# A two-layer decoder trunk on one Trainium2 core: where the first FFN's loop builds the S5 matrices

## The chip, the cores and the metric

The kernel runs on one core of one Trainium2 chip. The metric is the device time of one execution in microseconds. A core has five engines that run their own instruction streams and meet only at semaphores: TensorE (PE, with its weight loads as PEld), VectorE (DVE), ScalarE (ACT), GpSimd (POOL) and SyncE (SP).

## The reference, cut to what matters

Sixteen meta tokens are put ahead of 1024 tokens of width 1024, so T = 1040. Two layers follow, each with a mixer and a SwiGLU FFN, both between RMS norms. Layer 0 mixes with four gated-DeltaNet heads and four stick-breaking heads, layer 1 with a diagonal complex state-space model (S5) and a GLU.

```python
def swiglu_ffn(x, w_gate, w_up, w_down):
    return (jax.nn.silu(x @ w_gate) * (x @ w_up)) @ w_down

for i in range(DEPTH):
    hn = rms_norm(h, norm_mix_pre[i])
    m = deltanet_stickbreak_mixer(hn, ...) if i % 2 == 0 else s5_mixer(hn, ...)
    h = h + rms_norm(m, norm_mix_post[i])
    hn = rms_norm(h, norm_ffn_pre[i])
    h = h + rms_norm(swiglu_ffn(hn, ...), norm_ffn_post[i])
```

The FFN width is 2816. The S5 mixer has 64 groups of 16 channels, each driving 64 complex states. Its matrices (input and output matrices, phases, and the products of the two for each lag inside a chunk of 8 steps) depend on parameters alone, not on the tokens, so they can be built at any time before the mixer of layer 1.

## The kernel before, in words

Everything is written by engine: one function body each for SyncE, GpSimd, TensorE, ScalarE and VectorE, with the semaphores written out by hand. What an engine does, it does in the order of its body.

Activations lie feature-major, 128 features by T tokens, and the tokens are cut into three cuts of 352, 344 and 344 (CUTS). Each weight is streamed from HBM in slabs of 128 x 1024 (SyncE, L521) and split by GpSimd into a high and a low fp32r part (L554, L558); each product is three matmuls, high by high, high by low, low by high (L582 to L584).

The FFN goes over the 2816 hidden features in 11 turns (PAIRS) of two blocks of 128. A turn has six steps: step st works on cut st // 2 and block st % 2. On TensorE a step is `hidden(i, c, f)` with c = st // 2 and f = st % 2: the gate and up products of that block and cut, 48 matmuls into two of banks 0 to 3. ScalarE then takes silu of the gate (L1475), VectorE multiplies it by the up product (L2068), ScalarE copies that into act_hi (L1479), and VectorE makes act_lo of the rest (L2071). Behind the six steps TensorE makes the down products, `down(i, c)` for each cut, eight groups of six matmuls into three banks in turn (4, 5, 6); VectorE adds each group to acc (L2081) and so frees its bank.

The FFN of layer 0 (called with layer 0) carries the building of the S5 matrices. It has one channel tile (m = i - 1) in each of the turns i = 1 to 8 of its loop; the FFN of layer 1 has the same loop without it. Per turn:

- VectorE: behind step 0 `build_in` (the input matrices zb["m"], two parts), behind step 1 `build_out` (waits until the set of the turn before is stored), behind step 2 `build_phases`, behind step 5 `build_k`: it waits for the lag products in bank 7 and adds a diagonal term (L2198). The additions of the down products stand behind that.
- TensorE: `build_turn(m, 0)` transposes the first part into bank 7 (four transposes, L647), `build_turn(m, 1)` the second, `build_k` makes the lag products (eight matmuls of 32 columns, L655 and L656), all in bank 7. Each of the latter two waits for `s5["win"]`, that is, until ScalarE has evicted what bank 7 holds.
- ScalarE: `build_win(m, 0)` and `build_win(m, 1)` evict the transposed parts from bank 7 (L1493); the first also waits for the store of the set of the turn before. At the end of the turn `store_build` starts the DMA of the set (L1499) and eight DMAs of the lag products (L1501), and `load_tab` the next tables (L1486).

On TensorE the order of a turn is: groups 0, 1, 2, first transposes, group 3, second transposes, group 4, lag products, group 5, down products. On ScalarE the first eviction stands behind step 3, the second behind step 4.

Of the kernel before, what the change touches and what calls it, by code (L numbers as in the profile page):

```python
# [282 lines left out]
def trunk(nc, xT, wstream, small_in, const_in, s5_in, outT):  # L283
    with ExitStack() as ctx:
# [149 lines left out]
        def split_value(name, i, j):  # L434

            return first_slab(name) + i * len(slots_of(name)[1]) + j + 3
# [138 lines left out]
        def _(pe):  # L575
            mm = pe.matmul

            def gemm(out, slot, k, xk, cut, first, last, hi=x_hi, lo=x_lo):

                a, n = cut  # L580
                wk = slice(k * P, k * P + P)
                mm(out[:, 0:n], w_hi[:, slot, wk], hi[:, xk, a:a + n], start=first, stop=False)  # L582
                mm(out[:, 0:n], w_hi[:, slot, wk], lo[:, xk, a:a + n], start=False, stop=False)  # L583
                return mm(out[:, 0:n], w_lo[:, slot, wk], hi[:, xk, a:a + n], start=False, stop=last)  # L584
# [40 lines left out]
            def norm_sum(r, c, m):  # L625


                n = CUTS[c][1]
                e = norm_event(r, c, m)
                if e:  # L630
                    pe.wait_ge(nm_log, e)
                for k in range(KT):
                    if k % 4 == 0:

                        pe.wait_ge(nm_square, 2 * e + k // 4 + 1)
                    last = mm(norm_sums[:, 0:n], ones, nv["sq"][:, k, 0:n], start=(k == 0), stop=(k == KT - 1))  # L636
                last.then_inc(nm_sum, 1)
# [3 lines left out]
            def build_turn(m, part):  # L641

                if part == 0:
                    pe.wait_ge(s5["m"], m + 1)
                pe.wait_ge(s5["win"], 2 * m + part + 1)
                for q in range(QP):
                    last = pe.transpose(bank[7][:, q * P:q * P + P], zb["m"][part][:, q, :], ident)  # L647
                last.then_inc(s5["win_t"], 1)

            def build_k(m):  # L650

                pe.wait_ge(s5["win"], 2 * m + 3)
                for q in range(QP):
                    o = bank[7][:, q * 2 * G_CH:(q + 1) * 2 * G_CH]
                    mm(o, zb["m"][0][:, q, :], zb["cc"][0][:, q, :, :], start=True, stop=False)  # L655
                    last = mm(o, zb["m"][1][:, q, :], zb["cc"][1][:, q, :, :], start=False, stop=True)  # L656
                last.then_inc(s5["k"], 1)

            def ffn(layer, r):

                name = f"ffn{layer}"
                base = layer * PAIRS

                def hidden(i, c, f):

                    pe.wait_ge(split_done, split_value(name, i, 2 * f + 1))
                    step = (base + i) * 6 + 2 * c + f

                    pe.wait_ge(act_f32, step + 1)
                    for s in (2 * f, 2 * f + 1):  # L670
                        for k in range(KT):
                            last = gemm(bank[s], s, k, k, CUTS[c], k == 0, k == KT - 1)
                    last.then_inc(gu_done, 1)

                def down(i, c):

                    pe.wait_ge(split_done, split_value(name, i, 5))
                    pe.wait_ge(act_ready, (base + i) * 6 + 2 * c + 2)
                    for m in range(KT):
                        pe.wait_ge(down_free, (base + i) * 24 + c * 8 + m + 1)  # L680
                        b = bank[4 + (8 * c + m) % DOWN_BANKS]
                        slot = 4 + m // 4
                        for kk in range(2):
                            last = gemm(b, slot, kk * 4 + m % 4, kk, CUTS[c], kk == 0, kk == 1, act_hi, act_lo)
                        last.then_inc(down_done, 1)

                def pair(i):
                    for c in range(3):
                        hidden(i, c, 0)
                        hidden(i, c, 1)  # L690

                end = PAIRS - 1
                pe.wait_ge(x_ready, 3 * r + 1)
                hidden(0, 0, 0)
                norm_sum(r, 2, 0)
                hidden(0, 0, 1)
                pe.wait_ge(x_ready, 3 * r + 2)
                hidden(0, 1, 0)
                norm_sum(r, 2, 1)
                hidden(0, 1, 1)  # L700
                pe.wait_ge(x_ready, 3 * r + 3)
                hidden(0, 2, 0)
                hidden(0, 2, 1)
                for c in range(3):
                    down(0, c)
                with pe.Fori(1, end - 1) as i:
                    for c in range(3):
                        hidden(i, c, 0)
                        if layer == 0 and c == 1:
                            build_turn(i - 1, 0)  # L710
                        if layer == 0 and c == 2:
                            build_k(i - 1)
                        hidden(i, c, 1)
                        if layer == 0 and c == 1:
                            build_turn(i - 1, 1)
                    for c in range(3):
                        down(i, c)
                pair(end - 1)
                down(end - 1, 0)
                down(end - 1, 1)  # L720

                hidden(end, 0, 0)
                hidden(end, 0, 1)
                down(end - 1, 2)
                hidden(end, 1, 0)
                down(end, 0)
                hidden(end, 1, 1)
                norm_sum(r + 1, 0, 0)
                hidden(end, 2, 0)
                down(end, 1)  # L730
                if r + 1 < 4:
                    norm_sum(r + 1, 0, 1)
                hidden(end, 2, 1)
                norm_sum(r + 1, 1, 0)
                down(end, 2)
                if r + 1 == 4:
                    norm_sum(4, 2, 0)
# [339 lines left out]
        def _(act):  # L1077
# [7 lines left out]
            def norm_load(r, c):  # L1085

                a, n = CUTS[c]
                if r == 4 and c == 2:
                    act.wait_ge(nm_stored[0], 16 * 7)
                elif c == 2:  # L1090
                    act.wait_ge(x_ready, 3 * r + 1)
                elif r > 0:
                    act.wait_ge(x_ready, 3 * (r - 1) + (3 if c == 0 else 2))
                act.dma_start(nv["h"][c % 2][:, :, 0:n], stream_in[r][:, :, a:a + n]).then_inc(nm_loaded[c % 2], 16)
# [369 lines left out]
            def ffn(layer, r):  # L1464
# [19 lines left out]
                def load_tab(m):  # L1484

                    act.dma_start(zb["tab"], s5_tab[:, m, :]).then_inc(s5["tab_loaded"], 16)  # L1486

                def build_win(m, part):

                    act.wait_ge(s5["win_t"], 2 * m + part + 1)  # L1490
                    if part == 0:
                        act.wait_ge(s5["set_stored"], 16 * m + 16)
                    A(zb["win"][part].rearrange("p q s -> p (q s)"), bank[7], ACT.Copy).then_inc(s5["win"], 1)  # L1493
# [21 lines left out]
                if layer == 0:  # L1515
                    act.sem_inc(s5["win"], 1)
                    act.sem_inc(s5["set_stored"], 16)
                    act.sem_inc(s5["k_stored"], 16 * CH)
                    act.wait_ge(x_ready, 3 * r + 3)
                    load_tab(0)  # L1520
                    with act.Fori(1, end - 1) as i:
                        for st in range(6):
                            step(i, st)
                            if st in (3, 4):
                                build_win(i - 1, st - 3)
                        store_build(i - 1)
                        load_tab(i)
                    for st in range(3):
                        step(end - 1, st)
                    act.wait_ge(s5["set_stored"], 16 * KT + 16)  # L1530
                    act.wait_ge(s5["k_stored"], 16 * CH * (KT + 1))
                    act.wait_ge(s5["tab_loaded"], 16 * KT + 16)
                    norm_load(r + 1, 0)
                    norm_load(r + 1, 1)
                    for st in range(3, 6):
                        step(end - 1, st)
                else:
                    norm_load(r + 1, 0)
                    norm_load(r + 1, 1)
                    with act.Fori(1, end) as i:  # L1540
                        for st in range(6):
                            step(i, st)
# [28 lines left out]

            act.sem_inc(down_done, 1)
            ffn(0, 1)


# [806 lines left out]
```

## Time and profile before

| | us |
|---|---|
| median of 3 runs | 3452.55 |
| lowest and highest run | 3443.03, 3460.74 |
| span of the profiled execution | 3441.6 |
| TensorE busy | 2945.9 (86%) |
| VectorE busy | 1343.9 (39%) |
| GpSimd busy | 944.0 (27%) |
| ScalarE busy | 746.9 (22%) |

The profile records one execution; its span runs from the first to the last instruction. The granted TensorE clock is given as a share of full speed. The loop of the first FFN lies at about 1260 to 1895 us of the span, that of the second at about 2738 to 3290.

### The profile page before, as it was taken

How to read it: one execution, taken by the hardware profiler on the slowest of the kernel's cores; microseconds unless marked ns; L12 is line 12 of the kernel's file. 1: busy time of each engine (PE TensorE's matmuls, PEld its weight loads, DVE VectorE, ACT ScalarE, POOL GpSimd, SP SyncE). 2: the span in 40 equal slices, each digit the busy share in tenths (PEclk: the TensorE clock that was granted, in tenths of full speed). 3: DMA queues.
4: the chain of work that ended last, by engine and by line, in shares of the span. 5: the costliest groups of instructions: out<-in, count | busy, mean ns of one | idle time of the engine just before them, and what ended most of it. 6: DMA issues, size and time to landing. Idle time of an engine off the chain costs nothing.

```text
span 3441.6 us, 45325 instructions
## 1 busy us (share of the span) xinstructions
PE 2945.9 (86%) x17797; PEld 2782.7 (81%) x17797; DVE 1343.9 (39%) x2281; ACT 746.9 (22%) x1270; POOL 944.0 (27%) x390
## 2 busy tenths in 40 slices
PE   3999978776668899999999987755997999999996
PEld 2999966664448799999999986645996999999995
DVE  2664055544571544443434234063025332233223
ACT  3321133434562320000000033112033000000002
POOL 2344200000003333333434330400531544354430
PEclk8999988987778999999999998877998999999998
DMA  4222510000102211111122213686111211111101
GB/s 154 75 98 92 114 44 25 25 25 19 37 19 70 87 57 63 63 63 63 66 71 85 87 46 75 139 193 158 62 58 58 83 49 49 37 49 49 49 25 66
DMA packets 175482, 236.23 MB, mean 69 GB/s; under 512 B 56480, under 2 KB 140960, under 8 KB 173088
## 3 DMA queue, kind: packets, MB, share of 16 engines
q1 hardware_dynamic: 66064, 133.42, 13.0%
q10 hardware_dynamic: 109328, 101.54, 9.8%
q8 instruction: 65, 1.06, 0.1%
q14 instruction: 25, 0.20, 0.0%
HBM read 172.37 MB, written 62.55 MB: 68 GB/s over the span
## 4 chain that ended last, share of the span: by engine, by line
issue 34%; PE 32%; POOL 11%; DVE 9%; DMA 6%; ACT 5%; ACTq 2%; SPq 1%; POOLq 0%; DVEq 0%
POOL w_hi L554 7%; PE psum L582 7%; PE psum L583 6%; PE psum L584 6%; POOL w_lo L558 3%; DMA stage<-wstream 3%; PE psum L636 3%; DVE area L1701 2%; PE psum L825 2%; PE psum L817 1%; DVE area L2036 1%; PE psum L936 1%; DVE area L1706 1%; DMA area<-xT 1%; PE psum L833 1%
## 5 line engine op out<-in xcount | busy, mean ns | idle before, releaser
L582 PE MATMUL psum<-x_hi,w_hi 128*128 128x344 f32 (+2 forms) x3600 | 1176.8, 327 | 56.9 <-DVE x_lo L1724 34.3
L583 PE MATMUL psum<-x_lo,w_hi 128*128 128x344 f32 (+2 forms) x3600 | 1170.1, 325 | 0.0
L584 PE MATMUL psum<-x_hi,w_lo 128*128 128x344 f32 (+2 forms) x3600 | 1165.3, 324 | 0.0
L554 POOL TENSOR_TENSOR w_hi<-stage,const 128x1024 fp32r<-128x1024 f32 x193 | 471.8, 2445 | 2386.9 <-PE psum L584 2365.6
L582 PEld LDWEIGHTS psum<-x_hi,w_hi 128*128 128x128 f32 x3600 | 690.8, 192 | 62.3 <-DVE x_lo L1724 32.7
L583 PEld LDWEIGHTS psum<-x_lo,w_hi 128*128 128x128 f32 x3600 | 689.8, 192 | 1.9
L584 PEld LDWEIGHTS psum<-x_hi,w_lo 128*128 128x128 f32 x3600 | 690.8, 192 | 0.0
L558 POOL TENSOR_TENSOR w_lo<-stage,w_hi 128x1024 fp32r<-128x1024 f32 x193 | 475.8, 2465 | 15.1
L582 PE MATMUL psum<-act_hi,w_hi 128*128 128x344 f32 (+1 forms) x1056 | 347.8, 329 | 36.9 <-DVE area L2081 29.3
L2068 DVE TENSOR_TENSOR area<-area,psum 128x352 f32<-128x352 f32 (+1 forms) x132 | 68.0, 515 | 723.7 <-ACT area L1475 723.7
L584 PE MATMUL psum<-act_hi,w_lo 128*128 128x344 f32 (+1 forms) x1056 | 342.1, 324 | 0.0
L583 PE MATMUL psum<-act_lo,w_hi 128*128 128x344 f32 (+1 forms) x1056 | 341.3, 323 | 0.0
L1475 ACT ACTIVATE area<-psum 128x352 f32<-128x352 f32 (+1 forms) x132 | 60.7, 460 | 1280.0 <-PE psum L584 1280.0
L2081 DVE TENSOR_TENSOR area<-area,psum 128x344 f32<-128x344 f32 (+1 forms) x480 | 243.1, 515 | 187.2 <-PE psum L584 185.3
L582 PEld LDWEIGHTS psum<-act_hi,w_hi 128*128 128x128 f32 x1056 | 201.3, 191 | 45.4 <-DVE area L2081 36.4
L636 PE MATMUL psum<-area,const 128*128 128x344 f32 (+1 forms) x384 | 127.9, 491 | 89.8 <-ACT area L1111 89.8
L583 PEld LDWEIGHTS psum<-act_lo,w_hi 128*128 128x128 f32 x1056 | 203.4, 193 | 0.1
L584 PEld LDWEIGHTS psum<-act_hi,w_lo 128*128 128x128 f32 x1056 | 201.2, 191 | 0.0
L636 PEld LDWEIGHTS psum<-area,const 128*128 128x128 f32 x384 | 77.8, 207 | 132.0 <-issue 101.8
L1786 DVE TENSOR_TENSOR area<-area 128x512 f32<-128x512 f32 (+6 forms) x298 | 158.7, 587 | 40.6 <-ACT area L1240 32.4
L2071 DVE TENSOR_TENSOR act_lo<-area,act_hi 128x352 fp32r<-128x352 f32 (+1 forms) x132 | 103.4, 783 | 78.2 <-ACT act_hi L1479 78.2
L1701 DVE SCALAR_TENSOR_TENSOR area<-area,small 128x344 f32<-128x344 f32 (+1 forms) x96 | 73.8, 840 | 125.3 <-ACT area L1125 125.3
(214 smaller groups left out, 2571.8 us busy)
## 6 DMA issues: line engine op xcount, KB each, us to landing
stage<-wstream SPq DMA_DIRECT2D x193, 512.0 KB, 3.3
s_set<-area ACTq DMA_DIRECT2D x8, 1860.0 KB, 7.0
proj<-area ACTq DMA_DIRECT2D x28, 520.0 KB, 2.7
area<-proj ACTq DMA_DIRECT2D x40, 256.0 KB, 4.4
resid<-area ACTq DMA_DIRECT2D x6, 1376.0 KB, 6.0
area<-resid ACTq DMA_DIRECT2D x6, 1376.0 KB, 8.3
area<-proj ACTq DMA_DIRECT2D x12, 520.0 KB, 4.6
area<-xT ACTq DMA_DIRECT2D x4, 1376.0 KB, 8.3
```

What stands on the lines that cost most here:

```text
L554: pool.tensor_tensor(per_block(w_hi[:, slot, :]), per_block(stage[:, h, :]), all_ones, ALU.mult).then_inc(high_split, 1)
L558: pool.tensor_tensor(w_lo[:, slot, :], stage[:, h, :], w_hi[:, slot, :].bitcast(F32), ALU.subtract).then_inc(split_done, 1)
L582: mm(out[:, 0:n], w_hi[:, slot, wk], hi[:, xk, a:a + n], start=first, stop=False)
L583: mm(out[:, 0:n], w_hi[:, slot, wk], lo[:, xk, a:a + n], start=False, stop=False)
L584: return mm(out[:, 0:n], w_lo[:, slot, wk], hi[:, xk, a:a + n], start=False, stop=last)
L636: last = mm(norm_sums[:, 0:n], ones, nv["sq"][:, k, 0:n], start=(k == 0), stop=(k == KT - 1))
L825: last = mm(B[1][:, hs], v[s]["u"][:, hs], v[s]["t2"][:, hs], start=True, stop=True)
L1701: last = V.scalar_tensor_tensor(out=acc[:, k, a:a + n], in0=acc[:, k, a:a + n], scalar=small[:, at:at + 1], in1=rr, op0=mul, op1=mul)
L1786: tt = lambda o, a, b, op: ch(V.tensor_tensor(o, a, b, op))
L2068: V.tensor_tensor(f[st % 2][:, 0:n], gate[st % 2][:, 0:n], bank[2 * (st % 2) + 1][:, 0:n], mul).then_inc(act_f32, 1)
L2071: V.tensor_tensor(act_lo[:, st % 2, a:a + n], f[st % 2][:, 0:n], act_hi[:, st % 2, a:a + n].bitcast(F32), sub).then_inc(act_ready, 1)
L2081: last = V.tensor_copy(o, src) if first else V.tensor_tensor(o, o, src, add)
```

## The change

The first eviction on ScalarE moves from behind step 3 to behind step 2, the second from behind step 4 to behind step 3. On TensorE the lag products move from between groups 4 and 5 to behind group 5, ahead of the down products. The transposes stay where they are, and nothing is added or removed. Only the FFN of layer 0 is touched, and of it only the loop of eight turns.

```diff
@@ -708,11 +708,11 @@
                         hidden(i, c, 0)
                         if layer == 0 and c == 1:
                             build_turn(i - 1, 0)
-                        if layer == 0 and c == 2:
-                            build_k(i - 1)
                         hidden(i, c, 1)
                         if layer == 0 and c == 1:
                             build_turn(i - 1, 1)
+                    if layer == 0:
+                        build_k(i - 1)
                     for c in range(3):
                         down(i, c)
@@ -1521,8 +1521,8 @@
                     with act.Fori(1, end - 1) as i:
                         for st in range(6):
                             step(i, st)
-                            if st in (3, 4):
-                                build_win(i - 1, st - 3)
+                            if st in (2, 3):
+                                build_win(i - 1, st - 2)
                         store_build(i - 1)
                         load_tab(i)
```

## Rows read from the trace of the kernel before

**Rows 1.** The page's first row.
```profile
span 3441.6 us, 45325 instructions
```

**Rows 2.** Table by stretch: stretch, length, busy us (instructions) by engine, clock, DMA, GB/s.
```profile
1300.00:1895.00 595.00, 553.06 (x3427) 546.03 (x3426) 249.11 (x469) 51.61 (x108) 221.12 (x92) 0.97 0.20 69
2738.00:3290.00 552.00, 549.35 (x3459) 547.01 (x3459) 159.10 (x288) 45.97 (x97) 232.46 (x97) 1.00 0.14 46
```

**Rows 3.** The same for two turns; then line L1499, its issues: ns, first and last.
```profile
1494.80:1573.40 78.60, 73.36 (x459) 72.48 (x458) 33.47 (x64) 6.69 (x14) 28.90 (x13) 0.98 0.20 69
1573.40:1653.50 80.10, 74.86 (x457) 73.98 (x457) 33.40 (x64) 6.69 (x14) 28.76 (x13) 0.96 0.20 67
...
L1499 ACTq DMA_DIRECT2D s_set<-area x8: 362/362/377, 1335.7 to 1887.3; - x8
```

**Rows 4.** TensorE's waits, 1300 to 1895, then 2738 to 3290: us, times, longest.
```profile
PE psum L655 <- ACT area L1493: 17.4, 8, 2.2
PE psum L647 <- ACT area L1493: 16.8, 8, 2.1
PE psum L582 <- DVE area L2081: 7.7, 8, 1.0
...
PE psum L582 <- DVE area L2081: 2.7, 8, 0.3
```

**Rows 5.** Timeline of TensorE around the second transposes: start, length, idle before it.
```profile
1544.14 0.32 PE L584 MATMUL psum<-x_hi,w_lo 128*128 128x344 f32 x1
1546.56 0.66 PE L647 MATMUL psum<-const,area 128*128 128x128 f32 x4 [2.10 <-ACT area L1493]
1546.97 0.41 PE L582 MATMUL psum<-x_hi,w_hi 128*128 128x344 f32 x1
...
1547.85 0.49 PE L584 MATMUL psum<-x_hi,w_lo 128*128 128x344 f32 x1
...
1551.27 0.32 PE L584 MATMUL psum<-x_hi,w_lo 128*128 128x344 f32 x1
...
1551.90 0.32 PE L582 MATMUL psum<-x_hi,w_hi 128*128 128x344 f32 x1
```

**Rows 6.** Timeline of TensorE around the lag products.
```profile
1556.00 0.32 PE L584 MATMUL psum<-x_hi,w_lo 128*128 128x344 f32 x1
1558.50 0.41 PE L655 MATMUL psum<-area 128*128 128x32 f32 x2 [2.18 <-ACT area L1493]
...
1560.30 0.40 PE L582 MATMUL psum<-x_hi,w_hi 128*128 128x344 f32 x1
```

**Rows 7.** Timeline of TensorE, end of group 5 and the fourth down group.
```profile
1567.79 0.32 PE L584 MATMUL psum<-x_hi,w_lo 128*128 128x344 f32 x1
...
1570.71 0.32 PE L584 MATMUL psum<-act_hi,w_lo 128*128 128x352 f32 x1
...
1571.99 0.43 PE L582 MATMUL psum<-act_hi,w_hi 128*128 128x352 f32 x1 [0.96 <-DVE area L2081]
```

**Rows 8.** Timeline of ScalarE: copy of step 2, first eviction, silu of step 5.
```profile
1537.64 0.49 ACT L1479 ACTIVATE act_hi<-area 128x344 fp32r<-128x344 f32 x1 [0.66 <-DVE area L2068]
...
1545.93 0.58 ACT L1493 ACTIVATE area<-psum 128x512 f32<-128x512 f32 x1
...
1568.15 0.46 ACT L1475 ACTIVATE area<-psum 128x344 f32<-128x344 f32 x1 [9.70 <-PE psum L584]
```

**Rows 9.** Timeline of VectorE: output matrices, act_lo of step 5, first additions to acc.
```profile
1531.03 3.82 DVE L1786 TENSOR_TENSOR area<-area 128x512 f32<-128x512 f32 x6
...
1569.71 1.27 DVE L2071 TENSOR_TENSOR act_lo<-area,act_hi 128x344 fp32r<-128x344 f32 x1 [0.56 <-ACT act_hi L1479]
...
1571.42 1.38 DVE L2081 TENSOR_TENSOR area<-area,psum 128x352 f32<-128x352 f32 x3 [0.23 <-DVE area L2198]
```

**Rows 10.** Table by stretch, columns as in rows 2: short stretches of two turns.
```profile
1548.00:1550.00 2.00, 2.00 (x9) 2.00 (x8) 0.00 (x0) 0.00 (x0) 0.00 (x0) 0.50 0.00 0
...
1640.00:1643.40 3.40, 3.40 (x14) 3.40 (x13) 0.00 (x0) 0.00 (x0) 3.32 (x2) 0.50 0.48 154
```

## The prediction: what the change does to the time

> **What bounds the kernel now.** I read the page first: a span of 3441.6 us [rows 1]. Then the table by stretch for the loops of the two FFNs. They do the same matrix work in every turn, but only the first carries the S5 building. Over seven turns and a half of the first FFN TensorE is busy 553.06 of 595 us, with a clock of 0.97. Over eight turns of the second it is busy 549.35 of 552 us, with a clock of 1.00, so a turn there takes 69.0 us [rows 2]. The s5_set store is issued once a turn of the first FFN; from its first to its last issue (1335.7 to 1887.3) seven turns take 551.6 us, or 78.8 us each [rows 3]. A single turn takes 78.6 us, and one of them 80.1 us with a clock of 0.96 where the others have 0.98 [rows 3]. So TensorE is the bound of both loops, and a turn of the first is 9.8 us longer. The chain of the whole run names TensorE first; the other engines count here only where TensorE stands still for them.
>
> The view of waits says for whom. In the first FFN TensorE has three waits, each eight times: 17.4 us for the eviction at L1493 ahead of the lag products (L655), 16.8 us for the eviction at L1493 ahead of the second transposes (L647), 7.7 us ahead of a down product (L582) for VectorE's L2081. In the second FFN only the last is left, with 2.7 us [rows 4]. No wait for weights is there.
>
> **What the waits cost.** A matmul's end is modelled, so I count from start to start. Ordinary 344-column matmuls follow each other every 0.157 us (1551.27 to 1551.90, four steps [rows 5]).
> Second transposes: the last gate-and-up matmul starts at 1544.14, the first transpose at 1546.56: 2.42 − 0.16 = 2.26 us lost [rows 5].
> Lag products: 1556.00 to 1558.50: 2.50 − 0.16 = 2.34 us [rows 6].
> Fourth down group: 1570.71 to 1571.99: 1.28 − 0.16 = 1.12 us [rows 7].
> Clock: after the first of these gaps the granted clock falls to 0.50, its lower level of 1.2 GHz [rows 10]. From 1547.85 to 1551.27 TensorE starts 12 matmuls in 3.42 us, one per 0.285 us, where 12 at the upper level (2.4 GHz) take 1.88: 1.54 us lost [rows 5]. This happens in each of the eight turns; in the turn of 80.1 us the clock also falls after the lag products [rows 3, 10], and that turn is 1.5 us longer. So nine falls.
>
> **The change, part by part.**
> 1) The eviction of the first turned matrix goes from behind step 3 to behind step 2 on ScalarE. What it needs are the first transposes, which TensorE issues right behind the group of step 2 in both kernels. ScalarE starts step 2's copy at 1537.64, over a microsecond behind that group; the transposes, which hold TensorE for 0.41 us (1546.56 to 1546.97 for the second ones [rows 5]), are over by then. The copy ends at 1538.13, and the eviction takes 0.58 us: done at about 1538.8. TensorE wants it at 1544.3. So the wait of 2.26 us goes with 5.5 us to spare; today the eviction starts at 1545.93, because it stands behind silu, product and copy of step 3, that is, behind a group that TensorE has just finished [rows 5, 8]. The eviction costs ScalarE nothing: it has no other work until step 3's silu, which must wait for a group that ends at 1544.3.
> The eviction also waits for the s5_set store of the turn before, and now meets that wait one step earlier, with silu 3 queued behind it on ScalarE and step 3's product on VectorE behind that. VectorE's output matrices wait for the same store behind step 1, and start at 1531.03 without idling [rows 9]; the store is long done. Cost 0. From below zero nothing is to be had either.
> 2) The second eviction goes from behind step 4 to behind step 3. It needs the second transposes, which now follow step 3's group at once. It is done about 2.4 us behind that group (today: 1546.51, against a group that ended at 1544.30 [rows 5, 8]).
> 3) The lag products go from ahead of the last gate-and-up group to behind it. They find their matrix some 15 us old, so the wait of 2.34 us goes. The eight small matmuls cost the same 1.80 us (1558.50 to 1560.30 [rows 6]) wherever they stand.
> 4) What this does to the down products. Let H be the end of the last gate-and-up group, 1567.95 today (last start 1567.79 plus 0.16 [rows 7]; silu at 1568.15 [rows 8]). VectorE ends step 5 at 1569.71 + 1.27 = 1570.98, H + 3.0, sums the lag products, and adds three down results from 1571.42, H + 3.5 [rows 9]. The first is added at H + 4.0, and the fourth down group, which needs its bank, stands since H + 2.9. After the change TensorE spends H to H + 1.9 on the lag products, so the fourth group comes up at H + 4.8, behind the add at H + 4.0: the wait of 1.12 us goes too. VectorE now waits for fresh lag products: ready at H + 1.9 plus about 0.2 (the distance from H to silu), while VectorE is free for them at H + 3.0. Margin 0.9 us. The bounds of this item are 0 (all gone) and the whole 1.12 kept; I take 0, since the terms above leave 0.8 us.
> 5) DMAs. The store and the eight s5_k stores wait for the lag sum, which is bound by H + 3.0 in both kernels, so these and the table load behind them keep their place against H. No SyncE queue and no GpSimd instruction is moved. GpSimd may refill its first four slabs from steps 4 and 5 on; the two come 1.9 us closer together. It needs at most 20 us for them (29 us of work on six slabs a turn: 232.46 us in eight turns [rows 2]), and they are wanted only behind the down products, 24 groups of 6 matmuls or 23 us later. The second FFN runs this very order at 69.0 us a turn without a wait for weights [rows 2, 4]. Cost 0.
> 6) Clock. With the gaps gone nothing of the kind that precedes the falls is left: the loop of the second FFN, with a small gap of 0.3 us a turn, holds 1.00 throughout [rows 2, 4]. New is a stretch of 1.8 us with only small matmuls. Today the same stretch stands behind a gap of 2.34 us, and even together they brought a fall in one turn of eight. I take all nine falls as gone; the other end is that eight stay, 12.3 us.
> The Trainium skill, "TensorE: Matmul & The Clock Gate", section "Why this matters for your kernels", puts the danger at idle gaps longer than any of the three here. By it the falls would not come from the gaps, and the change would give back only 45.8 us; the trace of this kernel differs, with the clock at 0.50 right behind a gap of 2.26 us in every turn.
>
> **The sum.** Waits: 8 × (2.26 + 2.34 + 1.12) = 45.8 us. Clock: 9 × 1.54 = 13.9 us. Together 59.7 us, or 7.5 us a turn: 78.8 becomes 71.3. A check from the other side: the second FFN's 69.0, less its own 0.3 of waiting, plus 1.9 for the lag products and 2 × 0.45 for the transposes (0.41 from their first start to the next matmul [rows 5]) gives 71.5. The two agree within 0.2 us a turn.
> Against the profiled execution: 3441.6 − 59.7 = 3381.9 us of span. The runs gave 3443.0 to 3460.7, median 3452.6, which is 11.0 above that span. One profile doesn't show what makes the others longer; I suppose the same of the runs afterwards: 3452.6 − 59.7 = 3392.9 us.
>
> **Rivals.**
> A: the clock still falls once a turn, now behind the lag products or the transposes. For it: in one turn it fell behind the lag products, at 1640 [rows 10]. Against it: that was behind a gap that goes. Gain 45.8 + 1.5 = 47.3 us: 3405 us. Chance 0.13. The same page says, under "Part 4: PE-mode transpose", that transposes don't count as busy for the clock in the way other matmuls do; the trace has transposes right ahead of each of the eight falls, but never without the gap in front.
> B: the down wait stays, because VectorE is late with the sum (the lag products are now fresh and the margin is 0.9 us). Gain 59.7 − 9.0 = 50.7 us: 3402 us. Chance 0.05.
> C: the change doesn't do what it says: another semaphore of the same eviction comes last and both gaps merely move. ScalarE has the eviction at 1545.93 right behind its own copy, not behind something foreign, and VectorE's start at 1531.03 clears the store; both speak against it [rows 8, 9]. Time 3452. Chance 0.03.
> D, slower: VectorE now waits for lag products that are issued only behind the last group, and 24 additions to acc stand behind that wait; with three banks, TensorE's down products stop after three groups. The point: the sum may be late by 0.9 + 0.8 us for nothing; to eat the whole gain of 7.5 us a turn it would have to come 9.2 us late, and 11.3 us for a time 0.5% longer (17 us over 8 turns): 3470 us. It would need eight matmuls of 1.8 us to take over 13. Chance 0.02.
> The forecast itself has 0.77.
>
> **Range and chances.** From 3392.9, downward: the median before carries 11 us over the profiled span, and executions without it would give 3382; upward, A and B end at 3402 to 3405, and the spread of a median of a few runs is some 4 us on top. Range 3379 to 3409. Under 0.5%, or 17 us, a measurement of this kernel can't tell a change from none. Faster by more: the forecast, A and B, 0.95. Within: C, 0.03. Slower: D, 0.02.
>
> **What would show it.** The waits of TensorE for L1493 gone from the first FFN (34.2 us before); the wait for L2081 below 1 us in all; the s5_set stores 71.3 us apart; granted clock 1.00 in the loop's stretches; VectorE's L2198 starting about 3.0 us behind the last gate-and-up matmul, with no idle time ahead of it that ends on TensorE. It would be wrong if VectorE idles there for the lag products, if the clock falls behind them, or if ScalarE's silu 3 starts later against its group than 0.2 us.

## The result and the profile after

The changed kernel takes 3390.5 us (median of four runs, 3387.3 to 3392.9) against 3448.5 us for the kernel before on the same chip: 58 us less by the medians, and a ratio of 0.9825 (95% interval 0.9803 to 0.9847), which is 53 to 68 us. The second time it ran, on another occasion, the ratio was 0.985 (0.9828 to 0.9872), or 44 to 59 us. The profiled executions have spans of 3441.6 and 3385.5 us, 56.1 us apart.

The table by stretch of the changed kernel, for a stretch inside the loop of the first FFN and for eight turns of the second (stretch, length, then busy us and instructions of TensorE, its weight loads, VectorE, ScalarE, GpSimd, then the clock, the DMA share and GB/s):

```profile
1310.00:1820.00 510.00, 510.00 (x3274) 509.74 (x3273) 237.48 (x445) 49.25 (x103) 206.64 (x86) 1.00 0.22 74
2682.00:3234.00 552.00, 549.34 (x3459) 547.00 (x3458) 159.03 (x288) 45.96 (x97) 232.51 (x97) 1.00 0.14 46
```

TensorE is busy for all of 510 us, at the full clock, where it was busy 553 of 595 at 0.97 [rows 2]. The second FFN is as it was. The issues of the s5_set store, once a turn (ns; first and last start in us):

```profile
L1499 ACTq DMA_DIRECT2D s_set<-area x8: 362/362/377, 1329.5 to 1827.1; - x8
```

Seven turns take 497.6 us, or 71.1 us each, against 78.8 [rows 3]. So of the 56.1 us between the two spans 54.0 lie between the first and the last of these issues, and 6.2 ahead of the first, where the rest of the first turn is. Behind the last the changed kernel takes 4.1 us more (1558.4 against 1554.3 us). The view of waits of TensorE, 1230 to 1850 us, which holds the whole loop (who waits for whom: us in all, times, the longest):

```profile
PE psum L582 <- DVE x_lo L1724: 5.9, 1, 5.9
PE psum L582 <- DVE area L2081: 0.3, 1, 0.3
```

Both stand ahead of the loop of eight turns, at 1239.6 and 1259.6 us. The three groups of eight waits of [rows 4] are gone. The timeline of TensorE, first around the end of a turn's gate-and-up groups (start and length in us):

```profile
1539.20 0.32 PE L584 MATMUL psum<-x_hi,w_lo 128*128 128x344 f32 x1
1539.36 0.30 PE L655 MATMUL psum<-area 128*128 128x32 f32 x2
...
1541.06 0.41 PE L582 MATMUL psum<-act_hi,w_hi 128*128 128x352 f32 x1
...
1543.89 0.33 PE L584 MATMUL psum<-act_hi,w_lo 128*128 128x352 f32 x1
1544.06 0.33 PE L582 MATMUL psum<-act_hi,w_hi 128*128 128x352 f32 x1
...
1594.73 0.32 PE L584 MATMUL psum<-x_hi,w_lo 128*128 128x344 f32 x1
1594.89 0.60 PE L647 MATMUL psum<-const,area 128*128 128x128 f32 x4
1595.24 0.41 PE L582 MATMUL psum<-x_hi,w_hi 128*128 128x344 f32 x1
```

The lag products start 0.16 us behind the last gate-and-up matmul, take 1.70 us, and the fourth down group starts at 1544.06, 0.17 us behind the third. The second transposes (1594.89) follow group 3 without a gap. VectorE in the same places:

```profile
1541.11 1.15 DVE L2071 TENSOR_TENSOR act_lo<-area,act_hi 128x344 fp32r<-128x344 f32 x1 [0.56 <-ACT act_hi L1479]
1542.18 0.28 DVE L2198 TENSOR_TENSOR area<-psum,area 128x128 f32<-128x128 f32 x1
1542.69 1.11 DVE L2081 TENSOR_TENSOR area<-area,psum 128x352 f32<-128x352 f32 x2 [0.23 <-DVE area L2198]
```

The end of the last group, H, is 1539.20 + 0.16 = 1539.36. The lag sum starts at H + 2.8 right behind act_lo, without idling for TensorE. The first addition ends at about 1543.2, H + 3.9, and the bank it frees is wanted at H + 4.7. ScalarE, the first eviction of a turn and the next silu:

```profile
1588.23 0.49 ACT L1479 ACTIVATE act_hi<-area 128x344 fp32r<-128x344 f32 x1 [0.66 <-DVE area L2068]
1588.63 0.58 ACT L1493 ACTIVATE area<-psum 128x512 f32<-128x512 f32 x1
1595.08 0.46 ACT L1475 ACTIVATE area<-psum 128x344 f32<-128x344 f32 x1 [5.87 <-PE psum L584]
```

The eviction is over at 1589.2; TensorE wants it at 1594.9, and silu 3 starts 0.19 us behind its group (1594.73 + 0.16), so nothing is held up by the evictions.

### The profile page after: what moved, and what is told of

Same layout as the page of the kernel before. It is cut to its first block, busy times and chain, and to the rows that moved or that the text cites. A ratio compares the mean times of both kernels' runs of the same rounds, so it can differ in the third digit from the quotient of the medians.

```text
span 3385.5 us, 45325 instructions
## 1 busy us (share of the span) xinstructions
PE 2931.3 (87%) x17797; PEld 2770.2 (82%) x17797; DVE 1355.0 (40%) x2281; ACT 746.3 (22%) x1270; POOL 951.1 (28%) x390
## 4 chain that ended last, share of the span: by engine, by line
issue 34%; PE 28%; DVE 12%; POOL 11%; ACT 6%; DMA 6%; ACTq 2%; SPq 1%; POOLq 0%; DVEq 0%
POOL w_hi L554 7%; PE psum L582 5%; PE psum L583 5%; PE psum L584 5%; POOL w_lo L558 3%; DMA stage<-wstream 3%; PE psum L636 3%; DVE area L1778 2%; PE psum L825 2%; DVE area L1701 2%; PE psum L817 1%; DVE area L2036 1%; PE psum L936 1%; DVE area L1706 1%; PE psum L833 1%
## 5 line engine op out<-in xcount | busy, mean ns | idle before, releaser
L2081 DVE TENSOR_TENSOR area<-area,psum 128x344 f32<-128x344 f32 (+1 forms) x480 | 244.5, 514 | 191.7 <-PE psum L584 189.3
```

The lines of the kernel that those rows point to most:

```text
L2081: last = V.tensor_copy(o, src) if first else V.tensor_tensor(o, o, src, add)
```

## The experiments

All ratios are to the kernel before. "Turn" is the distance of the s5_set stores, from the first to the last of eight, over seven. "Falls" are stretches at the lower clock level, counted over the eight turns in the table by stretch, one row for each turn. In that table a turn without a fall has a clock of 1.00, one with a fall 0.98 and one with two 0.96; a fall on the boundary of two rows leaves 0.99 in both. Such a row counts the falls of a turn but doesn't tell behind which gap they come; that takes short stretches behind each gap. Line numbers are those of each kernel: an edit above a line shifts it.

For the kernel before, the prediction's rows have such stretches of two turns only, the fourth and the fifth [rows 5, 10]. Here are the first, second and sixth turn, for each the stretch behind the second transposes and then the one behind the lag products (the second line starts during the last lag products):

```profile
1311.00:1320.00 9.00, 7.94 (x52) 7.66 (x50) 0.51 (x1) 0.46 (x1) 0.98 (x1) 1.00 0.01 2
1322.60:1325.90 3.30, 3.30 (x14) 3.30 (x14) 0.00 (x0) 0.00 (x0) 3.30 (x2) 0.50 0.23 50
1390.90:1394.20 3.30, 3.30 (x13) 3.30 (x12) 0.00 (x0) 0.00 (x0) 0.00 (x0) 0.50 0.00 0
1403.00:1411.00 8.00, 8.00 (x53) 8.00 (x53) 0.00 (x0) 0.02 (x1) 5.92 (x3) 1.00 0.28 91
1706.00:1714.00 8.00, 7.48 (x48) 7.19 (x46) 0.00 (x0) 0.46 (x1) 0.44 (x1) 1.00 0.00 0
1718.50:1721.80 3.30, 3.30 (x13) 3.30 (x13) 0.00 (x0) 0.00 (x0) 3.22 (x3) 0.50 0.51 159
```

Read this way, the nine falls are four behind the second transposes (turns 2 to 5) and five behind the lag products (turns 1 and 5 to 8). The prediction had eight and one. Its count is right and its places are not, and the same misreading stands in the expectations of the next runs.

| kernel | turn us | TensorE waits left in the loop | falls | ratio (95%) |
|---|---|---|---|---|
| before | 78.8 | all three | 9 | 1 |
| changed | 71.1 | none | 0 | 0.9825 (0.9803 to 0.9847) |
| evictions only | 72.7 | L2081 | 0 | 0.9856 (0.982 to 0.9893) |
| lag products only | 74.7 | second transposes | 6 | 0.9927 (0.9898 to 0.9957) |
| first eviction only | 77.4 | lag products, L2081 | 13 | 0.9962 (0.9939 to 0.9985) |
| before, one gap filled | 78.8 | lag products, L2081 | 8 | 0.9999 (0.9977 to 1.0022) |
| before, both gaps filled | 77.1 | L2081 | 0 | 0.9969 (0.9955 to 0.9984) |
| changed, lag products twice | 73.7 | none | 4 | 0.9892 (0.9869 to 0.9915) |
| changed, one copy | 72.9 | L2081 | 0 | 0.9873 (0.9854 to 0.9892) |
| changed, four copies | 82.3 | L2081 | clock 0.94 | 1.0065 (1.0039 to 1.0091) |
| changed, sum three times | 71.1 | none | 0 | 0.9816 (0.9791 to 0.984) |
| changed, sum seven times | 72.3 | L2081 | 0 | 0.9854 (0.9831 to 0.9877) |
| changed, copies behind step 3 | 71.1 | none | 0 | 0.9833 (0.9811 to 0.9854) |

**The changed kernel again**, as the neighbour of the copies and the doubled lag products.

> The changed kernel itself, beside the next three on the same chip, as their reference: 3390 us, a gain of 56 to 60 us.

0.985 (0.9828 to 0.9872), or 52 us at 3452.0 us: a little less than the 56 to 60 expected. Its turn is 71.1 us again.

**The two halves of the change.** Evictions alone:

```diff
-                            if st in (3, 4):
-                                build_win(i - 1, st - 3)
+                            if st in (2, 3):
+                                build_win(i - 1, st - 2)
```

> Only ScalarE's part of the change: both evictions one step earlier, the lag products stay ahead of the last gate-and-up group. Theory (three waits and the clock falls behind them add up): TensorE's two waits for L1493 go, 8 x (2.26 + 2.34) = 36.8 us, the nine falls of the clock go with them, 13.9 us, the wait for L2081 stays (7.7 us in the view of waits). Gain 50.7 us against the kernel before, about 3398 us. Rival (the down wait has to do with the late evictions, not with the place of the lag products): it goes here too and the whole 59.7 us is gained. Rival (the clock falls come from the small matmuls, not from the gaps): gain 37 to 38 us, eight falls stay.

The lag products alone:

```diff
-                        if layer == 0 and c == 2:
-                            build_k(i - 1)
                         hidden(i, c, 1)
                         if layer == 0 and c == 1:
                             build_turn(i - 1, 1)
+                    if layer == 0:
+                        build_k(i - 1)
```

> Only TensorE's part of the change: the lag products behind the last gate-and-up group, the evictions where they were. Theory: the wait ahead of the lag products goes (8 x 2.34) and the wait for L2081 (8 x 1.12), the wait ahead of the second transposes stays (16.8 us) and with it one fall of the clock a turn. Gain 27.7 + 1.5 = 29.2 us, about 3419 us. Rival (the sum on VectorE is late for fresh lag products): L2081's wait stays, gain 20 us.

The waits of TensorE (evictions only; 1300 to 1840 us) and the stores:

```profile
PE psum L582 <- DVE area L2081: 9.7, 7, 1.4
...
L1499 ACTq DMA_DIRECT2D s_set<-area x8: 362/362/382, 1337.8 to 1847.0; - x8
```

The same of the kernel with the lag products moved only:

```profile
PE psum L647 <- ACT area L1493: 14.7, 7, 2.1
...
L1499 ACTq DMA_DIRECT2D s_set<-area x8: 362/362/382, 1342.8 to 1865.8; - x8
```

Each half removes the waits that the theory gives it and no other. The evictions alone end both waits for L1493 but leave the one for L2081; the lag products alone end that one and their own. The evictions bring 6.1 us a turn (8 × 6.1 = 49 us, expected 50.7; 50 us by the ratio), the lag products 4.1 (33 us, expected 29.2; 25 us by the ratio, with an interval of 15 to 35). In the first the down wait has even grown, to 1.4 us where it was 0.96: VectorE's act_lo of step 5 takes 1.69 us there, against 1.27 [rows 9]. The rival in which the down wait hung on the late evictions is out, and so is a late lag sum. In the second six turns of eight still have a fall, all behind the second transposes: three falls fewer than before, where the theory had one fewer. That is most of the 4 us above the expectation.

**The first eviction alone**, where only the wait ahead of the second transposes goes:

```diff
-                            if st in (3, 4):
-                                build_win(i - 1, st - 3)
+                            if st in (2, 4):
+                                build_win(i - 1, st // 2 - 1)
```

> Only the first eviction one step earlier; the second stays behind step 4 and the lag products ahead of the last group. Theory: the wait ahead of the second transposes goes, 8 x 2.26 = 18.1 us, and the eight falls behind it, 12.3 us; the gap of 2.34 us ahead of the lag products and L2081's wait stay. If that gap brings a fall of its own no more often than before (one turn in eight), the gain is 30 us, about 3418 us; if it brings one in each turn, 18 to 20 us. The granted clock by turn tells which.

The gain is 13 us, not 18 to 32, and by the turn 8 × 1.4 = 11. Two of its turns in the table by stretch (the clock is the third number from the end):

```profile
1336.10:1413.50 77.40, 74.68 (x456) 74.18 (x456) 33.13 (x63) 6.70 (x14) 28.25 (x13) 0.96 0.21 70
1490.90:1568.30 77.40, 73.68 (x460) 72.78 (x458) 34.31 (x66) 6.70 (x14) 29.87 (x14) 0.98 0.21 70
```

Five turns have 0.96 and three 0.98: thirteen falls where the kernel before has nine. All thirteen come behind the gap ahead of the lag products, at least one in each turn. Neither expected outcome came: with the first gap gone, the second brings one or two falls in a row. It all adds up nevertheless: 78.8 less the gap of 2.26, with 13 falls instead of 9 over eight turns (+0.5 × 1.54 = 0.8), is 77.3, and 77.4 was measured.

**One gap filled, then both.** This keeps every microsecond of waiting but gives TensorE something to do in it:

```diff
                         hidden(i, c, 1)
                         if layer == 0 and c == 1:
+                            pe.wait_ge(down_free, i * 24 + DOWN_BANKS)
+                            for _n in range(14):
+                                mm(bank[4][:, 0:344], w_hi[:, 0, 0:P], x_hi[:, 0, 352:696], start=True, stop=True)
                             build_turn(i - 1, 1)
```

> The kernel before, with 14 matmuls of 344 columns into an idle bank put on TensorE between group 3 and the second transposes; their results are used by nothing. They take 14 x 0.157 = 2.2 us, the length of the gap. So the gap is filled with work and not a microsecond of waiting is saved. Theory (the gap makes the clock fall): the eight falls behind the second transposes go and nothing else, gain 12.3 us, about 3436 us. Rival (the transposes or the turn's rhythm make it fall, not the gap): no fall goes, no gain.

The ratio is 0.9999: no gain. Timeline of TensorE with the gap filled, and two short stretches of the same turn behind it:

```profile
1552.26 2.36 PE L717 MATMUL psum<-x_hi,w_hi 128*128 128x344 f32 x14
1554.52 0.65 PE L647 MATMUL psum<-const,area 128*128 128x128 f32 x4
1564.91 0.41 PE L655 MATMUL psum<-area 128*128 128x32 f32 x2 [2.18 <-ACT area L1496]
```

```profile
1564.30:1567.70 3.40, 2.79 (x22) 2.79 (x23) 1.12 (x1) 0.56 (x2) 3.32 (x2) 1.00 0.00 0
1567.80:1571.20 3.40, 3.40 (x14) 3.40 (x14) 0.00 (x0) 0.00 (x0) 3.32 (x2) 0.51 0.49 154
```

The fall behind the second transposes is gone as the theory said, but all eight falls now come behind the lag products, where the kernel before has five. They are not one a turn: the first turn has none, the second has two in a row (6.8 us at 0.50), the other six one each. So four falls went and three came. I changed the theory: either gap by itself brings a fall a turn, and the clock comes back only when both go. The second filler stands ahead of the lag products, in addition to the first:

```diff
                         if layer == 0 and c == 2:
+                            for _n in range(15):
+                                mm(bank[4][:, 0:344], w_hi[:, 2, 0:P], x_hi[:, 0, 352:696], start=True, stop=True)
                             build_k(i - 1)
```

> The kernel before with both gaps filled: 14 matmuls of 344 columns ahead of the second transposes, as with one gap filled, and 15 more (2.35 us) ahead of the lag products; their results are used by nothing. No waiting is saved, TensorE only works through it. Theory, as it stands after the run with one gap filled (either gap by itself brings one fall of the clock a turn; the falls go only when both are gone): all falls of the loop go, gain 9 x 1.54 = 13.9 us, about 3438 us, with a turn of 77.0 us. Rival (the small matmuls bring the falls, whatever stands ahead of them): falls stay, no gain.

```profile
L1504 ACTq DMA_DIRECT2D s_set<-area x8: 362/362/378, 1343.3 to 1882.8; - x8
...
1340.00:1860.00 520.00, 513.25 (x3269) 509.17 (x3268) 232.74 (x439) 45.46 (x95) 192.63 (x80) 1.00 0.21 71
```

These are its stores and its row in the table by stretch. The turn is 539.5 / 7 = 77.1 us, where 77.0 was expected, the clock holds 1.00, and the ratio of 0.9969 is 11 us. That is the part of the gain that is the clock's, by itself. The seven turns between the stores have eight of the nine falls of the kernel before and are 551.6 − 539.5 = 12.1 us shorter, 1.51 us for a fall, or 13.6 us for nine, against the 13.9 of the prediction.

**The lag products twice**, for the stretch of small matmuls:

```diff
-                for q in range(QP):
+                for q in 2 * tuple(range(QP)):
```

> The changed kernel with the eight lag matmuls issued twice, sixteen in a row, 3.6 us, the second time over the first with the same values. Theory: TensorE pays 8 x 1.8 = 14.4 us. VectorE gets the lag products at H + 3.8 instead of H + 3.0 (H is the end of the last gate-and-up group), but TensorE reaches its fourth down group 1.8 us later too, so no wait comes in: about 3405 us. Theory of the clock (only gaps make it fall): it holds 1.00. Rival (small matmuls count as little as a gap): a fall in each turn, 12 us more, 3417 us.

```profile
1700.23 0.30 PE L655 MATMUL psum<-area 128*128 128x32 f32 x2
...
1703.52 0.62 PE L656 MATMUL psum<-area 128*128 128x32 f32 x2
1703.95 0.64 PE L582 MATMUL psum<-act_hi,w_hi 128*128 128x352 f32 x1
```

```profile
1703.50:1706.90 3.40, 3.40 (x14) 3.40 (x14) 0.81 (x2) 0.00 (x0) 3.32 (x2) 0.50 0.82 316
```

The first are rows of its TensorE timeline, the last one of its table by stretch. TensorE never waits, as expected, yet the clock falls behind the sixteen small matmuls (here 1700.23 to 1703.95) in four of the eight turns. The truth lies between the two expectations, also by the medians (18 us above the changed kernel in the same comparison, expected 14 or 26): the turn is 2.6 us longer, 1.8 for the matmuls and 0.8 for half a fall a turn. So small matmuls can bring a fall with no gap at all, which was rival A's mechanism; the eight small matmuls of the changed kernel, 1.7 us, bring none in any of its eight turns. Wherever a gap of 2.3 us stands in these kernels, transposes or lag products follow it at once, so no run shows what such a gap does by itself.

**The margin of the lag sum.** The late sum is rival D's mechanism, so I delayed it. With n copies ahead of it (here one; in this diff and in the next two on VectorE the constant BUILD_MARKS, the number of marked VectorE instructions in a turn, is raised by what is added, which is not shown):

```diff
             def build_k(m):
 
+                for _n in range(1):
+                    ch.sync()
+                    ch(V.tensor_copy(zb["tmp"][0][:, 0:512], zb["tmp"][1][:, 0:512]))
                 dve.wait_ge(s5["k"], m + 1)
```

> The changed kernel with one more copy of 128x512 (0.43 us and a semaphore, some 0.55 us) on VectorE ahead of the lag sum in each of the eight turns. Theory: the first addition to acc may come 0.8 us later than now before TensorE's fourth down group waits for it, so this costs nothing: the time of the changed kernel, no wait of TensorE for L2081. Rival (the margin is used up already): 8 x 0.55 = 4.4 us slower than the changed kernel.

> The same with four copies, some 2.1 us a turn. Theory: 0.8 us of it is covered, the rest makes TensorE wait for L2081 in each turn: 8 x 1.3 = 10 us slower than the changed kernel, about 3400 us; a gap of 1.3 us is no longer than the 1.12 us that went without a fall of the clock, so no fall. Rival (no margin): 17 us slower.

Both were far off: by the medians, 14 and 77 us above the changed kernel of the same comparison, where 0 and 10 were expected. Rows of the first (the copy, and TensorE around its fourth down group), then the four copies in the timeline of the other. In these two kernels L2198 is the copy:

```profile
1558.34 1.15 DVE L2071 TENSOR_TENSOR act_lo<-area,act_hi 128x344 fp32r<-128x344 f32 x1 [0.56 <-ACT act_hi L1479]
1559.41 2.61 DVE L2198 COPY area<-area 128x512 f32<-128x512 f32 x1
...
1561.12 0.32 PE L584 MATMUL psum<-act_hi,w_lo 128*128 128x352 f32 x1
1563.03 0.43 PE L582 MATMUL psum<-act_hi,w_hi 128*128 128x352 f32 x1 [1.59 <-DVE area L2081]
```

```profile
1581.47 10.06 DVE L2198 COPY area<-area 128x512 f32<-128x512 f32 x4
...
1586.24 2.52 POOL L554 TENSOR_TENSOR w_hi<-stage,const 128x1024 fp32r<-128x1024 f32 x1
1588.84 2.40 POOL L558 TENSOR_TENSOR w_lo<-stage,w_hi 128x1024 fp32r<-128x1024 f32 x1
```

A copy takes 2.6 us, not 0.43, and four take 10 us, about one for each instruction of GpSimd. Read with the true delay, one copy agrees with the theory: 2.5 us more on VectorE, and TensorE's fourth down group starts 1.75 us late (1561.12 + 0.16 to 1563.03), so 0.78 us was covered. With four, TensorE waits 9.0 us a turn, the clock is at 0.50 for 10.2 us of it, and the turn grows by 11.2 us (stretch from its table, then its waits of TensorE, 1300 to 1840 us):

```profile
1586.20:1596.40 10.20, 3.86 (x13) 3.87 (x14) 7.36 (x8) 0.00 (x0) 4.96 (x3) 0.50 0.59 193
```

```profile
PE psum L582 <- DVE area L2081: 63.2, 7, 9.0
```

That kernel is slower than the one before: 1.0065. Two doubts remained, the copy and the margin.

For the copy: four of them behind step 3, where GpSimd has no weights to split.

```diff
                             if st == 2:
                                 build_phases(i - 1)
+                            if st == 3:
+                                for _n in range(4):
+                                    ch.sync()
+                                    ch(V.tensor_copy(zb["tmp"][0][:, 0:512], zb["tmp"][1][:, 0:512]))
```

> The changed kernel with the four copies of 128x512 put behind step 3 on VectorE, where GpSimd is idle, instead of ahead of the lag sum, where it splits weights. Theory (a copy from SBUF to SBUF on VectorE waits for GpSimd's instruction to end): here each takes 0.43 us, and all are done before step 4, so no cost: a turn of 71.1 us. Rival (such a copy takes 2.4 us by itself, whatever GpSimd does): four take 10 us, which delays step 4's product and makes TensorE wait.

```profile
L2112 DVE COPY area<-area x32: 418/427/428, 1336.1 to 1835.1; 128x512 f32<-128x512 f32 x32
...
L1499 ACTq DMA_DIRECT2D s_set<-area x8: 362/362/378, 1352.9 to 1850.5; - x8
```

0.43 us each (ns, shortest, median and longest), and a turn of 497.6 / 7 = 71.1 us: the copies are free there. It was GpSimd, which has no instruction there. The Trainium skill, "SBUF — State Buffer", section "Who interferes with whom", says that such a copy and a GpSimd instruction exclude each other from a shared port for as long as an instruction lasts. By that rule a copy beside back-to-back GpSimd work costs one of its instructions, 2.4 us, and the rows agree: 10.06 us for four copies, with GpSimd instructions of 2.52 and 2.40 us beside them.

For the margin: the sum itself repeated, which reads PSUM.

```diff
-                ch(V.tensor_tensor(zb["k"], bank[7][:, 0:P], zb["dd"].rearrange("p g c -> p (g c)"), add))
-                ch.sync()
+                for _n in range(3):
+                    ch(V.tensor_tensor(zb["k"], bank[7][:, 0:P], zb["dd"].rearrange("p g c -> p (g c)"), add))
+                    ch.sync()
```

> The changed kernel with VectorE's lag sum (L2198) made three times in a row instead of once, to the same values. It reads PSUM, so it keeps its 0.28 us beside GpSimd's work, where a copy from SBUF to SBUF took 2.6 us. Two more cost about 2 x 0.35 = 0.7 us with their semaphores. Theory (margin of the first addition 0.75 to 0.8 us): no cost, a turn of 71.1 us, no wait for L2081 over 0.1 us. Rival (no margin, any delay of the sum is paid): 8 x 0.7 = 5.6 us.

> The same made seven times, six more, 6 x 0.35 = 2.1 us. Theory: 0.8 us is covered, 1.3 us is a wait of TensorE for L2081 in each turn, so a turn of 72.4 us, 10.6 us more in all than the changed kernel, and the clock holds 1.00. Rival (no margin): 16.8 us more.

```profile
L1499 ACTq DMA_DIRECT2D s_set<-area x8: 362/362/377, 1337.6 to 1835.0; - x8
```

```profile
1553.22 2.23 DVE L2199 TENSOR_TENSOR area<-psum,area 128x128 f32<-128x128 f32 x7
...
PE psum L582 <- DVE area L2081: 8.0, 8, 1.0
...
L1499 ACTq DMA_DIRECT2D s_set<-area x8: 362/362/377, 1338.8 to 1845.2; - x8
```

Three sums: a turn of 497.4 / 7 = 71.1 us, no cost (the fence above). Seven (the fence below it: timeline, waits, stores): 2.23 − 0.28 = 1.95 us more on VectorE, 1.25 us more a turn (72.34 against 71.09), so 0.70 us covered. The rival that any delay is paid falls twice.

## Why the prediction was right

**The three waits.** 2.26, 2.34 and 1.12 us of [rows 5 to 7] are gone from the changed kernel, and the halves take away just the ones named. The turn came out at 71.1 us where the sum gave 71.3 and the second FFN's check 71.5. This part was right in mechanism and in size.

**The clock.** 13.9 us were put down to nine falls, and all nine are gone. Filling both gaps gives this term alone, 13.6 us. The size was right, the reading behind it wrong: I tied eight falls to the gap ahead of the second transposes and one to the lag products, after short stretches of two turns. They are four and five. So the reason in item 6, that the lag products brought a fall in one turn of eight even behind a gap, does not hold: they did in five. Rival A had more for it than I gave it, and that no fall stayed in the full change was in this respect luck. In the full change the places make no difference, since both gaps go; for either half they do. Which of two gaps brings the fall in a given turn, and why the second alone brings 13 falls with the first eviction moved and 8 with the first gap filled, the runs don't settle.

**The lag products in their new place.** They take 1.70 us up to the first down product; the sum is not late. The margin was put at 0.8 us and measures 0.70 to 0.78 us in two independent ways. Rival B, the down wait that stays, did not occur. Rival D is real as a mechanism: it needs a sum 9.2 us late to eat the gain by the prediction, and four copies, 10 us, made a kernel slower than the one before. D's sum left out the clock: by it 10.1 us cost 0.9 us a turn against the kernel before, and 3.5 were measured, with the clock at 0.50 for 10.2 us of each turn.

**Rival A** (falls from the small matmuls) got 0.13. It did not occur in the profiled executions, but with the products doubled it did: the mechanism exists, and this kernel doesn't reach it. The Trainium skill, "TensorE: Matmul & The Clock Gate", section "Why this matters for your kernels", weighed in the prediction, puts the danger at longer gaps than these. By it filling the gaps would have given nothing; filling both gave 1.7 us a turn. The Trainium skill, "TensorE: Matmul & The Clock Gate", section "Part 4: PE-mode transpose", says that transposes don't count as busy in the same way. Without a gap they brought nothing here: in the changed kernel, and with the gap ahead of the second ones filled, no fall comes behind a transpose. The prediction's sentence that the trace has transposes right ahead of each of the eight falls holds for four of nine.

**Queues and DMAs**: costed at nothing. The stores keep their place and no wait for weights appears in the loop.

**The total.** 59.7 us were forecast, 3392.9 us. The loop of eight turns gives 8 × 7.7 = 61.7 us by the turn; the profiled spans differ by 56.1: the part behind the loop, untouched by the change, took 4.1 us more and what lies ahead of the loop 1.5 us (6.2 us less up to the first store, of which one turn gives 7.7). Neither is put down to the change: over all profiled executions the part behind the last store takes 1553.4 to 1559.8 us, and in the four with a turn of 71.1 us the first store comes anywhere from 1329.5 to 1352.9 us. The medians of the first comparison differ by 58 us; the forecast lies inside its interval and just above that of the second (44 to 59 us).

## What to carry to other kernels

Where one engine is always busy but for a few waits on evictions, look at which instruction the eviction stands behind: if its data are ready a step earlier, moving it costs nothing and returns the wait in full. Count the gap from start to start of the matmuls, and add the clock that the gap costs, but credit the clock only if no other gap of the kind stays in the loop. Look for the lower clock behind every gap of every turn: a mean over a turn counts the falls and doesn't place them. Before work is moved in front of an engine's queue of frees, work out how late it may come, and price the neighbours' operations beside what GpSimd is doing at that time.

## What was not expected of the hardware

- Two gaps of 2.3 us a turn, with transposes behind one and small matmuls behind the other, brought nine falls of the clock in eight turns, four behind the first gap and five behind the second. With the first gap filled there were eight, with the first eviction alone moved thirteen, all behind the second; with the lag products alone moved six, behind the first.
- Gaps of 1.1 to 1.75 us ahead of down products, counted from start to start, brought none.
- Sixteen small matmuls of 32 columns without any gap let the clock fall to 0.50 in four turns of eight; eight of them (1.7 us) in none.
- A copy of 128x512 from SBUF to SBUF on VectorE takes 0.43 us with GpSimd idle and 2.4 to 2.6 us beside its weight splitting. The sum that reads PSUM keeps its 0.28 us.
